# Moving latent rotations, filler units and a key norm in a two-block transformer kernel

## The chip, the core and the metric

The kernel runs on one core of one Trainium2 chip, in one launch. The metric is the device time of a launch in microseconds, median of several runs. Five engines work side by side: TensorE (matmuls, transposes), VectorE, ScalarE, GpSimd and SyncE, which here issues the weight loads. They meet at semaphores only, and each runs its own instructions in order.

## The reference

Two transformer blocks follow each other on 256 tokens of width 2048, all in float32.

- First block: RMS norm, one wide projection, then two attentions side by side. The *compressed/selected/window* attention has 16 query heads in 4 groups of 96 columns, with keys and values shared in a group. The *latent* attention has 16 heads: its queries come from a normed latent of 512 columns through `mla_w_uq`, keys and values from one of 256 columns through `mla_w_uk` and `mla_w_uv`; the last 32 of a head's 96 query columns are rotated by position, and one rotated key part of 32 columns is shared by all heads. Both results are gated and projected; then cross attention to a memory, and a feed-forward part.
- Second block: again a norm and a wide projection; an attention of 8 heads whose queries and keys are normed per head and then rotated, a retention of 8 heads, projections, a gated feed-forward part and a last gated term.

```
q = (rmsnorm(c_q, g_q) @ w_uq).reshape(b, s, MLA_HEADS, MLA_NOPE + MLA_ROPE)
q_rope = apply_rope(q[..., MLA_NOPE:], cos, sin)
k_nope = (ckv @ w_uk).reshape(b, s, MLA_HEADS, MLA_NOPE)
k_r = apply_rope(k_rope, cos, sin)
...
ak = rotate_half_split(heads(rms_norm(ak.reshape(B, T, ATTN_HEADS, HEAD_DIM), k_norm[i])...), pos, inv_freq_attn)
```

## The kernel before

**Matrix products.** Weights arrive in groups of 1 MB (4 row tiles of 128 by 512 columns), 469 in all. For each, ScalarE makes a rounded copy `whi` (`conv`, L1352) and VectorE the rest `wlo` (L1807); two groups fit in `whi` and `wlo`, four in `raw`. TensorE multiplies three times (activation high and low by `whi`, L692 and L693, then high by `wlo`, L697): 24 matmuls of 512 columns per group. Results go to two accumulators `acc`, taken out by ScalarE (`take`, L1385) or VectorE; `acc_free` counts what has been taken. `taken_by(eng, c)` waits until chunk c is out. So each of the three engines has a fixed program in which a group's conversion alternates with other steps; a step is hung in front of a conversion by a hook number.

**Ahead of the first attention.** Three chunks of latent queries `qm` (`C_UQ` to `C_UQ + 2`) are taken by ScalarE, each behind a conversion. Then come two groups of double width, latent keys `kcat` and values `vm`: the first half of each is taken by ScalarE (`two`), the second by VectorE (`second_half`, L1985), which converts a group behind each. `kr_rope` (L1974) rotates the shared key part.

**First attention.** `plan_items` lists 44 items: *prep* (transposes of queries or keys of a group of heads, L923), *attn* (scores of two heads, L941, then exponentials on ScalarE, L1573, transposes of probabilities, L960, value products, L996) and *cmp* (compressed part). Items 3 to 8 are the first group of heads, 9 to 15 the second, 16 to 22 the third, 23 to 29 the fourth (each begins with a prep of the next but one), 30 to 43 the latent heads. TensorE's, ScalarE's and VectorE's programs walk the same list: in step m they do the front of item m, the transposes of item m - 2 and the value products and outputs of item m - 3 (`DEPTH = 3`). A prep or a score product may overwrite its accumulator only once the item two fronts earlier is released; the first two wait for the chunks of `vm` instead.

Between items TensorE gets *filler units*: a projection that has nothing to do with the attention, cut into 32 units of six matmuls of 256 columns (`unit`, L881). `fill_plan` says how many units follow which item. Eight units use up one weight group; when its last unit is done, ScalarE and VectorE convert the group after next in two halves (`conv_half`), in the two items that follow. On VectorE `attend` also runs `mla_operands` (L2002) ahead of three items, 17, 19 and 21:

```
qr = qm[:, :, :].rearrange("p t (h d) -> p t h d", d=DK)
if t < TT:
    for c in (C_UQ + 1, C_UQ + 2):
        taken_by(dve, c)
    c_, s_ = (cs[n][:, t:t + 1, :].to_broadcast([P, HEADS, bh]) for n in ("cosb", "sinb"))
    rope(qr[:, t, :, NOPE:NOPE + bh], qr[:, t, :, NOPE + bh:DK], c_, s_, scratch(rtmp2, HEADS, bh))
    return
linked()
dve.wait_ge(mm_done, 35)
V.tensor_copy(kcat[:, :, :, NOPE:DK], kr.unsqueeze(2).to_broadcast([P, TT, HEADS, ROPE])).then_inc(mla_ready, 1)
```

A rotation (`rope`) is six instructions, L1869 to L1875. The first latent prep is item 23 and waits for `mla_ready`.

**Second block.** The projection's chunks c = 2 to 13 of four groups each carry steps of VectorE, numbered n = 4 c + j: the table `norms` (L2416) hangs `head_product` (squares), `head_sums` (sum, mean, reciprocal) and `norm2` on them. `norm2` has four steps: times the root, times the gain, rotation of tokens 0 to 127, rotation of tokens 128 to 255. Queries are n = 20 to 23, keys 24 to 27. ScalarE takes the root in between (`qk_root`). At n = 28 TensorE transposes the first two heads (`moba_turn`, L1184, L1169), which waits for `qk_ready`, set by the last rotations.

## Time and profile before

| what | value |
|---|---|
| median of 3 runs | 2829.67 us (2828.91 to 2829.94) |
| profiled execution | 2828.72 us, its span 2826.9 us |
| TensorE matmul busy | 2807.8 us, 99% |
| VectorE, ScalarE busy | 1476.9 us (52%), 1223.3 us (43%) |
| mean granted clock of TensorE | 0.995 |
| whole conversion, ScalarE and VectorE | 1.92 us, 2.29 us |
| half conversion, ScalarE and VectorE | 1.07 us, 1.22 us |
| copy of the shared key part (L2013) | 0.69 us |

Three views are used. The list of waits says for which instruction of which engine another one waited. The timeline shows instructions in order of time; in brackets stands how long the engine had been idle and what released it. Windows sum the busy time of each engine between two times and give TensorE's granted clock as a share of 2.4 GHz, so that 0.50 is its lower level of 1.2 GHz. All times count from the span's start.

### The profile page before, as it was taken

The page shows a single profiled execution, that of the slowest core. Times are in us where ns is not written, and L with a number is a line of the kernel's source. Part 1 is how long each engine was busy: PE and PEld are TensorE (multiplying, and loading weights), DVE is VectorE, ACT ScalarE, POOL GpSimd, SP SyncE. Part 2 cuts the span into 40 slices and gives each one's busy share as a digit, 9 for nine tenths or more (in the row PEclk, how much of TensorE's full clock was granted, in tenths as well). Part 3 has the DMA queues.
Part 4 walks back from the last instruction along what each step waited for, and adds up shares of the span by engine and source line. Part 5 has one row for each costly group of instructions (what it writes and reads, how often), then busy time and mean ns, then how long its engine had stood idle before and what let it go on. Part 6 is the DMA issues. An engine that isn't in the chain of part 4 may idle for free.

```text
span 2826.9 us, 32393 instructions
## 1 busy us (share of the span) xinstructions
PE 2807.8 (99%) x13433; PEld 2347.7 (83%) x13433; DVE 1476.9 (52%) x1187; ACT 1223.3 (43%) x1271; POOL 14.7 (1%) x28
## 2 busy tenths in 40 slices
PE   9999999999999999999999999999999999999999
PEld 7888898888888888888888888888888888888887
DVE  4445655445555544454455675665545444445555
ACT  5436454445554334343344544344433333333443
POOL 0000000000000000000000000000000000000000
PEclk9999999999999999999999999999999999999999
DMA  7745015556555565555655654545655555555554
GB/s 253 218 133 179 31 54 185 193 188 215 179 164 181 191 193 182 193 190 190 193 182 186 216 193 148 171 157 179 212 186 187 193 193 193 186 193 188 192 179 149
DMA packets 256429, 508.00 MB, mean 180 GB/s; under 512 B 8163, under 2 KB 18993, under 8 KB 255409
## 3 DMA queue, kind: packets, MB, share of 16 engines
q1 hardware_dynamic: 254112, 495.61, 53.5%
q0 software_dynamic: 2016, 10.36, 1.1%
q8 instruction: 95, 1.56, 0.2%
q10 hardware_dynamic: 176, 0.23, 0.0%
q14 instruction: 30, 0.24, 0.0%
HBM read 504.08 MB, written 2.10 MB: 179 GB/s over the span
## 4 chain that ended last, share of the span: by engine, by line
PE 86%; DVE 1%; ACT 0%; issue 0%; ACTq 0%
PE acc L692 26%; PE acc L693 26%; PE acc L697 26%; PE tb L678 2%; PE tb L996 1%; PE acc L941 1%; PE tb L1179 0%; ACT whi L1352 0%; DVE wlo L1807 0%; PE tb L960 0%; PE acc L894 0%; PE acc L891 0%; PE acc L893 0%; PE tb L1169 0%; PE acc L923 0%
## 5 line engine op out<-in xcount | busy, mean ns | idle before, releaser
L1807 DVE TENSOR_TENSOR wlo<-raw,whi 128x2048 fp32r<-128x2048 f32 (+1 forms) x465 | 1064.8, 2290 | 1228.6 <-ACT whi L1352 1228.4
L1352 ACT ACTIVATE whi<-raw 128x2048 fp32r<-128x2048 f32 (+1 forms) x465 | 890.4, 1915 | 1471.6 <-PE acc L697 1465.9
L692 PE MATMUL acc<-whi,ahi 128*128 128x512 f32 (+1 forms) x1968 | 770.0, 392 | 0.4 <-DVE alo L1899 0.4
L693 PE MATMUL acc<-whi,alo 128*128 128x512 f32 (+1 forms) x1968 | 764.2, 389 | 0.0
L692 PE MATMUL acc<-whi,bhi 128*128 128x512 f32 x1528 | 597.3, 391 | 0.5 <-DVE blo L1837 0.3
L693 PE MATMUL acc<-whi,blo 128*128 128x512 f32 x1528 | 594.7, 389 | 0.0
L697 PE MATMUL acc<-wlo,ahi 128*128 128x512 f32 (+1 forms) x1968 | 484.2, 387 | 0.0
L692 PEld LDWEIGHTS acc<-whi,ahi 128*128 128x128 f32 x1968 | 372.0, 189 | 76.0 <-DVE wlo L1896 0.9
L693 PEld LDWEIGHTS acc<-whi,alo 128*128 128x128 f32 x1968 | 372.0, 189 | 74.4
L697 PEld LDWEIGHTS acc<-wlo,ahi 128*128 128x128 f32 x1968 | 367.1, 188 | 75.5
L697 PE MATMUL acc<-wlo,bhi 128*128 128x512 f32 x1528 | 377.8, 389 | 0.0
L692 PEld LDWEIGHTS acc<-whi,bhi 128*128 128x128 f32 x1528 | 286.9, 188 | 60.7 <-DVE blo L1837 1.2
L697 PEld LDWEIGHTS acc<-wlo,bhi 128*128 128x128 f32 x1528 | 286.8, 188 | 59.6
L693 PEld LDWEIGHTS acc<-whi,blo 128*128 128x128 f32 x1528 | 287.0, 188 | 58.6
L1862 DVE TENSOR_TENSOR h<-acc,h 128x1024 f32<-128x1024 f32 x40 | 48.7, 1218 | 6.4 <-PE acc L697 6.4
L692 PE MATMUL acc<-whi,mhi 128*128 128x512 f32 x128 | 50.2, 392 | 0.0
L693 PE MATMUL acc<-whi,mlo 128*128 128x512 f32 x128 | 49.8, 389 | 0.0
L941 PE MATMUL acc<-kT,qT 96*128 96x128 f32 (+1 forms) x192 | 46.4, 363 | 1.8 <-ACT prob L1573 1.8
L1573 ACT ACTIVATE prob<-acc,negmax 128x128 f32<-128x128 f32 x96 | 39.0, 420 | 8.3 <-DVE negmax L2039 8.3
L2039 DVE TENSOR_REDUCE negmax<-acc 128x2 f32<-128x256 f32 (+1 forms) x48 | 25.2, 554 | 25.9 <-PE acc L944 25.9
L1541 ACT ACTIVATE probT<-tb 128x384 f32<-128x384 f32 x24 | 11.8, 491 | 56.5 <-PE tb L960 56.5
L1406 ACT ACTIVATE junk<-h 128x512 bf16<-128x512 f32 x56 | 35.5, 633 | 1.2
(341 smaller groups left out, 1592.0 us busy)
## 6 DMA issues: line engine op xcount, KB each, us to landing
raw<-in_w_ff SPq DMA_DIRECT2D x128, 1024.0 KB, 5.1
raw<-in_w_in SPq DMA_DIRECT2D x119, 1024.0 KB, 5.1
raw<-in_w_gate SPq DMA_DIRECT2D x44, 1024.0 KB, 5.1
raw<-in_w_up SPq DMA_DIRECT2D x44, 1024.0 KB, 5.1
raw<-in_w_down SPq DMA_DIRECT2D x44, 1024.0 KB, 5.0
raw<-in_w_out SPq DMA_DIRECT2D x16, 1024.0 KB, 5.1
raw<-in_w_o SPq DMA_DIRECT2D x16, 1024.0 KB, 5.0
raw<-in_w_ple_gate SPq DMA_DIRECT2D x16, 1024.0 KB, 5.1
```

The costliest lines, as they stand in the source:

```text
L678: last = nc.tensor.transpose((into or tb[w.n["turn"] % 2])[:, n * P:(n + 1) * P], src, ident)
L692: nc.tensor.matmul(out_(t), hi[:, kt, tt(t)], whi[:, slot, wc(k)], start=first and k == 0, stop=False)
L693: nc.tensor.matmul(out_(t), lo[:, kt, tt(t)], whi[:, slot, wc(k)], start=False, stop=False)
L697: mm = nc.tensor.matmul(out_(t), hi[:, kt, tt(t)], wlo[:, slot, wc(k)], start=False, stop=last and k == len(kts) - 1)
L941: nc.tensor.matmul(o[:, at:end], q[:, t * P:(t + 1) * P], k[:, 0:nk], start=True, stop=False)
L996: last = nc.tensor.matmul(o, probT[:, p % 2, n, b * P:(b + 1) * P], value_of(it, hd, BLOCKS[f][b][1]), start=b == bs[0], stop=b == bs[-1])
L1352: nc.scalar.activation(whi[:, g % SPLIT, 0:n_], raw[:, g % RAW, 0:n_], ACT.Copy).then_inc(w_hi, 1)
L1406: nc.scalar.activation(junk[:, 0:src.shape[-1]], src, ACT.Square, accum_out=ssq[:, r, t, n:n + 1]).then_inc(ssq_done, 1)
L1573: last = nc.scalar.activation(prob[:, p % 2, n, at:end], s[:, n * COLS + c0:n * COLS + c1], ACT.Exp, bias=negmax[:, p % 2, n * TT + t:n * ...
L1807: V.tensor_tensor(wlo[:, g % SPLIT, 0:n_], raw[:, g % RAW, 0:n_], whi[:, g % SPLIT, 0:n_].bitcast(F32), ALU.subtract).then_inc(w_lo, 1)
L1862: V.tensor_tensor(h[:, :, col(n)], v2(s[:, :]), h[:, :, col(n)], ALU.add).then_inc(done, 1)
L2039: last = V.tensor_reduce(negmax[:, p % 2, :].rearrange("p (n t) -> p n t", t=TT)[:, :, t], src, AX.X, ALU.max, negate=True)
```

## The change

Six edits, none of which alters a computed value; the instructions are the same but for their order and waits.

1. `fill_plan`: two units are put behind item 4, those behind items 33 and 37 go. Groups of units thereby end at items 5, 15 and 29 instead of 7, 19 and 33, and half conversions follow them.
2. ScalarE takes the third chunk of `qm` ahead of a conversion instead of behind it (`early`).
3. The latent queries are rotated ahead of the attention: tokens 0 to 127 between the two `second_half` calls, tokens 128 to 255 behind the second.
4. The copy of the shared key part into `kcat` follows its rotation at once.
5. TensorE's first latent prep waits for two counts of `mla_ready`, one from each rotation.
6. `norms`: squares and sums of the keys move from n = 17 and 18 to 16 and 17, query steps from 20 to 23 to 19 to 22, key steps from 24 to 27 to 23 to 26; `qk_root` moves with them.

```diff
--- before.py
+++ after.py
@@ -456,9 +456,9 @@
 
             plan = {m: 1 for m in calls[0] if m < 2 or items[m]["kind"] != "prep"}
             last = calls[0][-1]
-            for m in (last - 15, last - 16, last - 4, last - 2):
+            for m in (last - 15, last - 16, last - 10, last - 6, last - 4, last - 2):
                 del plan[m]
-            plan.update({2: 2, last + 1: 1, last + 2: 1})
+            plan.update({2: 2, 4: 2, last + 1: 1, last + 2: 1})
             assert sum(plan.values()) == FILL_UNITS - 2
             return plan
 
@@ -1014,7 +1014,7 @@
 
                 pe.wait_ge(o_done, items[-1]["u"] + 1)
 
-            attend({("nsa", "q"): (cmp_in, 2), ("mla", "q"): (mla_ready, 1)})
+            attend({("nsa", "q"): (cmp_in, 2), ("mla", "q"): (mla_ready, 2)})
 
 
             def turn_chunk(src, n, c=None, extra=None):
@@ -1484,7 +1484,7 @@
                          3: lambda: (root(R_CQ), root(R_CKV))},
                      ev=lambda: take(lambda t: ga0[:, t, :], ACT.Sigmoid, R_X))
             for n in range(3):
-                block_of(1, ev=lambda: take(lambda t: qm[:, t, col(n)], r=R_CQ))
+                block_of(1, ev=lambda: take(lambda t: qm[:, t, col(n)], r=R_CQ), early=n == 2)
             for t in range(TT):
                 last = nc.scalar.activation(gsig[:, t, :, :].rearrange("p h b -> p (h b)"),
                                             qkv[:, t, O_GN:O_GN + 3 * HEADS], ACT.Sigmoid)
@@ -1738,7 +1738,7 @@
             for c in range(2, 12):
                 hooks = {j: lambda n=4 * c + j: pair_step(n) for j in range(4)}
                 if c == 4:
-                    hooks[3] = qk_root
+                    hooks[2] = qk_root
                 block_of(4, hooks, lambda: take(lambda t: z[:, t, col(c)], r=R_Z))
             for j in range(2):
                 hooks = {i: lambda n=4 * (12 + j) + i: pair_step(n) for i in range(4)}
@@ -1974,6 +1974,9 @@
             def kr_rope():
                 taken_by(dve, 8)
                 rope(kr[:, :, 0:bh], kr[:, :, bh:ROPE], cs["cosb"], cs["sinb"], scratch(rtmp, TT, bh))
+                linked()
+                dve.wait_ge(cmp_h, 2)
+                V.tensor_copy(kcat[:, :, :, NOPE:DK], kr.unsqueeze(2).to_broadcast([P, TT, HEADS, ROPE]))
 
             block_of(2, {1: cmp_out})
             block_of(4, {1: lambda: turn(chi, clo, 0, 4, gT2[:, 0:4]),
@@ -1996,23 +1999,19 @@
                 w.n["used"] += 1
                 w.n["chunk"] += 2
 
+            def query_latent_rope(t):
+
+                qr = qm[:, :, :].rearrange("p t (h d) -> p t h d", d=DK)
+                for c in (C_UQ, C_UQ + 1, C_UQ + 2):
+                    taken_by(dve, c)
+                c_, s_ = (cs[n][:, t:t + 1, :].to_broadcast([P, HEADS, bh]) for n in ("cosb", "sinb"))
+                rope(qr[:, t, :, NOPE:NOPE + bh], qr[:, t, :, NOPE + bh:DK], c_, s_, scratch(rtmp2, HEADS, bh),
+                     by=(mla_ready, t + 1))
+
             second_half(lambda t: kcat[:, t, 8:16, 0:NOPE], R_CKV, lambda s: s.rearrange("p (h d) -> p h d", d=NOPE))
+            query_latent_rope(0)
             second_half(lambda t: vm[:, t, col(1)], R_CKV)
-
-            def mla_operands(t):
-
-                qr = qm[:, :, :].rearrange("p t (h d) -> p t h d", d=DK)
-                if t < TT:
-                    for c in (C_UQ + 1, C_UQ + 2):
-                        taken_by(dve, c)
-                    c_, s_ = (cs[n][:, t:t + 1, :].to_broadcast([P, HEADS, bh]) for n in ("cosb", "sinb"))
-                    rope(qr[:, t, :, NOPE:NOPE + bh], qr[:, t, :, NOPE + bh:DK], c_, s_, scratch(rtmp2, HEADS, bh))
-                    return
-                linked()
-                dve.wait_ge(mm_done, 35)
-                V.tensor_copy(kcat[:, :, :, NOPE:DK], kr.unsqueeze(2).to_broadcast([P, TT, HEADS, ROPE])
-                              ).then_inc(mla_ready, 1)
-
+            query_latent_rope(1)
 
             def o_view(it):
 
@@ -2131,13 +2130,11 @@
                     ins.then_inc(w_lo, 1)
                 w.n["group"] += half
 
-            def attend(between):
+            def attend():
 
                 ms = calls[0]
                 deep = DEPTH
                 for m in range(ms[0], ms[-1] + 1 + deep):
-                    if m in between:
-                        between[m]()
                     if m <= ms[-1]:
                         front_of(m)
                     for step, k in ((end_of, m - deep), (middle_of, m - deep + 1)):
@@ -2150,9 +2147,7 @@
                     if m - 2 in FILL_ENDS:
                         conv_half(1, FILL_ENDS[m - 2])
 
-            at = next(m for m in calls[0] if items[m]["kind"] == "attn" and items[m]["g"] == 2)
-            attend({at + 2 * t: lambda t=t: mla_operands(t) for t in range(TT + 1)})
-
+            attend()
 
             def gates(i, last=False):
                 out_ = lambda: mixed[:, :, col(i) if isinstance(i, int) else ds(i * COLS, COLS)]
@@ -2413,14 +2408,13 @@
                 if n in R_B and R_B[n] < PAIRS:
                     ret_decay(R_B[n])
 
-            norms = {4 * 5 + j: lambda j=j: norm2(0, j) for j in range(4)}
-            norms.update({4 * 6 + j: lambda j=j: norm2(1, j) for j in range(4)})
+            norms = {4 * 4 + 3 + j: lambda j=j: norm2(j // 4, j % 4) for j in range(8)}
             norms.update({
                 4 * 2 + 1: lambda: (dve.wait_ge(con2_in, 16 * 3), taken_by(dve, C_IN2), taken_by(dve, C_IN2 + 1),
                                     head_product(0)),
                 4 * 2 + 2: lambda: head_sums(qss[:, 0, :]),
-                4 * 4 + 1: lambda: (taken_by(dve, C_IN2 + 2), taken_by(dve, C_IN2 + 3), head_product(1)),
-                4 * 4 + 2: lambda: head_sums(qss[:, 1, :], qk_var),
+                4 * 4: lambda: (taken_by(dve, C_IN2 + 2), taken_by(dve, C_IN2 + 3), head_product(1)),
+                4 * 4 + 1: lambda: head_sums(qss[:, 1, :], qk_var),
                 4 * 9 + 2: lambda: (taken_by(dve, C_IN2 + 6), taken_by(dve, C_IN2 + 7), rope2(3, "r", 3, 0)),
                 4 * 9 + 3: lambda: rope2(3, "r", 3, 1),
                 4 * 10 + 1: lambda: (taken_by(dve, C_IN2 + 8), taken_by(dve, C_IN2 + 9), rope2(4, "r", 4, 0)),
```

VectorE, ahead of the first attention (`kcat` latent keys, `vm` latent values, `qm` latent queries, `rtmp` scratch). Before:

```order
L1807 TENSOR_TENSOR wlo<-raw,whi 128x2048 x4
L1993 TENSOR_SCALAR kcat<-acc,rstd 128x8x64 x2
L1807 TENSOR_TENSOR wlo<-raw,whi 128x2048
L1993 TENSOR_SCALAR vm<-acc,rstd 128x512 x2
L1807 TENSOR_TENSOR wlo<-raw,whi 128x2048
L2039 TENSOR_REDUCE negmax<-acc 128x2
```

and after the change:

```order
L1979 COPY kcat<-qkv 128x32x32
L1807 TENSOR_TENSOR wlo<-raw,whi 128x2048 x4
L1996 TENSOR_SCALAR kcat<-acc,rstd 128x8x64 x2
L1807 TENSOR_TENSOR wlo<-raw,whi 128x2048
L1869 TENSOR_TENSOR rtmp_130<-qm,con 128x256
L1870 TENSOR_TENSOR rtmp_130<-qm,con 128x256
L1871 TENSOR_TENSOR rtmp_130<-qm,con 128x256
L1872 TENSOR_TENSOR rtmp_130<-qm,con 128x256
L1874 TENSOR_TENSOR qm<-rtmp_130 128x16x16
L1875 TENSOR_TENSOR qm<-rtmp_130 128x16x16
L1996 TENSOR_SCALAR vm<-acc,rstd 128x512 x2
L1807 TENSOR_TENSOR wlo<-raw,whi 128x2048
```

Six instructions of a rotation stand ahead of the values' copy, and the key copy ahead of the four conversions.

VectorE, opening of the second block's attention (`z` the projection, `negmax` the first maximum of scores). Before:

```order
L1874 TENSOR_TENSOR z<-tmp_98 128x8x64
L1875 TENSOR_TENSOR z<-tmp_98 128x8x64
L1807 TENSOR_TENSOR wlo<-raw,whi 128x2048
L2349 TENSOR_REDUCE negmax<-tb 128x2 x2
L1807 TENSOR_TENSOR wlo<-raw,whi 128x2048 x2
L2356 COPY pT_103<-tb 128x384
L2349 TENSOR_REDUCE negmax<-tb 128x2 x2
L1807 TENSOR_TENSOR wlo<-raw,whi 128x2048
```

and after the change:

```order
L1874 TENSOR_TENSOR z<-tmp_98 128x8x64
L1875 TENSOR_TENSOR z<-tmp_98 128x8x64
L1807 TENSOR_TENSOR wlo<-raw,whi 128x2048 x2
L2344 TENSOR_REDUCE negmax<-tb 128x2 x2
L1807 TENSOR_TENSOR wlo<-raw,whi 128x2048 x2
L2351 COPY pT_103<-tb 128x384
L2344 TENSOR_REDUCE negmax<-tb 128x2 x2
L1807 TENSOR_TENSOR wlo<-raw,whi 128x2048
```

Behind the last rotation there are now two conversions ahead of the first maximum instead of one: the rotation has moved up by a group.

## Rows read from the trace of the kernel before

**Rows 1.** Page, busy totals; TensorE's waits: us in total, times, longest

```profile
PE 2807.8 (99%) x13433; PEld 2347.7 (83%) x13433; DVE 1476.9 (52%) x1187; ACT 1223.3 (43%) x1271; POOL 14.7 (1%) x28
...
PE tb L1169 <- DVE z L1875: 3.3, 1, 3.3
...
PE tb L996 <- DVE probT L2064: 2.9, 4, 1.9
...
PE tb L996 <- DVE qkv L2117: 1.8, 2, 1.3
...
PE acc L941 <- ACT prob L1573: 1.8, 1, 1.8
```

**Rows 2.** First attention, windows: busy us (x instructions) by engine, granted clock, DMA

```profile
281.60:288.52 6.92, 6.92 (x43) 6.53 (x44) 2.68 (x9) 2.81 (x12) 0.00 (x0) 0.75 0.01 2
295.59:305.33 9.74, 9.06 (x73) 8.10 (x71) 7.90 (x19) 5.70 (x18) 0.00 (x0) 1.00 0.32 98
305.33:311.22 5.89, 5.51 (x45) 4.95 (x44) 3.77 (x13) 2.40 (x10) 0.00 (x0) 1.00 0.06 19
346.30:355.37 9.07, 9.07 (x76) 8.53 (x75) 5.83 (x17) 4.77 (x16) 0.00 (x0) 1.00 0.19 75
295.59:318.29 22.70, 21.64 (x171) 19.50 (x170) 15.31 (x41) 11.24 (x42) 0.00 (x0) 1.00 0.15 47
318.29:346.30 28.01, 24.83 (x170) 22.15 (x169) 20.23 (x54) 13.02 (x45) 0.00 (x0) 0.88 0.05 15
375.88:379.90 4.02, 4.02 (x34) 3.71 (x34) 2.68 (x7) 1.71 (x7) 0.00 (x0) 1.00 0.00 0
391.78:395.33 3.55, 3.46 (x29) 2.93 (x28) 2.09 (x5) 1.27 (x5) 0.00 (x0) 1.00 0.00 0
```

**Rows 3.** The same view at the opening of the second block's attention

```profile
1709.36:1717.32 7.96, 7.96 (x32) 6.58 (x33) 2.18 (x1) 1.08 (x2) 0.00 (x0) 0.79 0.51 169
1724.55:1731.56 7.01, 7.01 (x39) 6.03 (x38) 2.76 (x2) 3.26 (x4) 0.00 (x0) 1.00 0.50 168
1725.42:1725.99 0.57, 0.57 (x8) 0.57 (x7) 0.00 (x0) 0.57 (x1) 0.00 (x0) 1.00 1.04 406
```

**Rows 4.** Timelines there: start, us, instruction, [idle before it <- releaser]

```profile
1709.36 1.14 PE L1169 MATMUL tb<-con,z 128*128 128x128 f32 x8 [3.28 <-DVE z L1875]
...
1642.85 2.29 DVE L1807 TENSOR_TENSOR wlo<-raw,whi 128x2048 fp32r<-128x2048 f32 x1 [3.15 <-ACT whi L1352]
...
1648.29 2.29 DVE L1807 TENSOR_TENSOR wlo<-raw,whi 128x2048 fp32r<-128x2048 f32 x1 [3.15 <-ACT whi L1352]
...
1708.53 0.68 DVE L1875 TENSOR_TENSOR z<-tmp 128x512 f32<-128x512 f32 x1
...
1642.72 1.24 ACT L1385 ACTIVATE z<-acc,rstd 128x512 f32<-128x512 f32 x2
```

**Rows 5.** Timelines, opening of the first attention: TensorE, then VectorE

```profile
262.85 0.50 PE L692 MATMUL acc<-whi,chi 128*128 128x512 f32 x1 [0.50 <-ACT qm L1385]
...
272.83 0.64 PE L923 MATMUL acc<-con,qkv 128*96 128x128 f32 x4
...
274.30 1.08 PE L923 MATMUL acc<-con,qkv 128*96 128x128 f32 x8
...
278.41 0.36 PE L891 MATMUL tb<-whi,ahi 128*128 128x256 f32 x1
...
279.21 0.60 PE L923 MATMUL acc<-con,qkv 128*96 128x128 f32 x4
...
267.93 2.29 DVE L1807 TENSOR_TENSOR wlo<-raw,whi 128x2048 fp32r<-128x2048 f32 x1 [0.60 <-ACT whi L1352]
...
271.37 1.41 DVE L1993 TENSOR_SCALAR vm<-acc,rstd 128x512 f32<-128x512 f32 x2 [1.14 <-PE acc L697]
...
322.03 0.41 DVE L1869 TENSOR_TENSOR rtmp<-qm,con 128x256 f32<-128x256 f32 x1
...
324.17 0.42 DVE L2039 TENSOR_REDUCE negmax<-acc 128x2 f32<-128x256 f32 x1
```

## The prediction

> **What bounds the kernel now.** I read the totals first: TensorE carries matmuls in 99% of the span [rows 1]. What a re-ordering can win is the time in which TensorE stands still, and what each such pause does to its clock afterwards. So the second view is the list of TensorE's waits [rows 1]: four entries hold 9.8 us, and each lies where the change works. 3.3 us: the first transposes of the second block's attention (L1169) wait for the last rotation of its keys on VectorE (L1875). 2.9 and 1.8 us: value products of the first attention (L996) wait for VectorE. 1.8 us: a score product (L941) waits for ScalarE's exponentials. There is more than the waits: TensorE's granted clock is 1.00 in most stretches, but 0.75 in the one that begins behind the 1.8 us pause, at 281.60 [rows 1, 2], 0.88 in the third group of heads [rows 2] and 0.79 behind the 3.28 us pause at 1709.36 [rows 3, 4]. These are mixtures of its two levels, 2.4 and 1.2 GHz: TensorE stood, and its clock then fell for some us. A stall is therefore priced as a difference between two stretches with the same instructions, one with and one without it. Ends of windows are starts of TensorE instructions.
>
> **Second block, key norm a group earlier.** A group of weights (24 matmuls of 512 columns) takes 5.44 us, the distance of two conversions on VectorE [rows 4], which converts one per group and does its steps in between. The last key rotation starts its last instruction at 1708.53 and TensorE starts at 1709.36 [rows 4]. All steps from the squares of the keys on move up by one group, so this end moves from 1709.2 to about 1703.8, ahead of 1706.1, where TensorE stood ready (1709.36 less 3.28). What could stop it is the input: the step now at hook 16 needs the second key columns out of the accumulator. ScalarE starts that copy at 1642.72 and is done by 1644.0; VectorE comes to the hook at 1642.85 + 2.29 = 1645.1 [rows 4]. It is there with 1.1 us to spare. Gain: the pause, 3.28, and the clock. From the transposes to the next score product it is 7.96 us at clock 0.79; the same for the next pair is 7.01 at 1.00, in which six more transposes take 0.57 [rows 3]: 7.96 - (7.01 - 0.57) = 1.52. Together **4.8 us**. Nothing new is late: the weight conversion behind the rotation starts at 1703.8 and its product comes two thirds through a group that now begins at 1706.9.
>
> **First attention, latent query copy ahead of a conversion.** ScalarE's third copy goes ahead of a 1.9 us conversion, and the 0.50 us pause at 262.85 [rows 5] ends. The conversion is 1.2 us later, for a group that TensorE wants only at 265.2, after about 262.7. Gain 0.5, carried into the next term.
>
> **First attention, opening.** VectorE now rotates half of the latent queries between conversion and value copy. The conversion starts at 267.93, by the term before at about 267.4, ends 2.29 later at 269.7; the rotation takes 324.17 - 322.03 = 2.14 and a wait for its own write of 0.1, so the value copy that started at 271.37 starts at 271.9 [rows 5]. TensorE's second preparation (keys, 272.83) follows the copy by 1.46: 273.4, a **new wait** of about 1.1 us. The third one stood before for ScalarE and absorbs a part: 274.30 becomes 274.5 [rows 5]. From there on all is 0.2 late, the score product at 281.60 too, with two more filler units in front of it that eat most of its pause (a unit is six matmuls, 279.21 - 278.41 = 0.80 with the switch [rows 5]). From it to the next score product it was 6.92 at clock 0.75; the twin in the second group of heads needs 5.89 at 1.00, with a wait of its own [rows 2]. 5.89 is what I take: 281.8 + 5.89 = 287.7 against 288.52, gain **0.8**, though two units more are done. The second rotation and the key copy (0.69, formerly in the attention) lie in VectorE's idle time and cost nothing. If the copy waited a full rotation, and nothing absorbed it, it would cost 1.6 more; if the third preparation absorbed all, 0.2 less.
>
> A rule weighed against this row: successive rotation instructions start 0.34 apart though each is shown with 0.42, six in 2.14 us [rows 5]. The Trainium skill, VectorE: DVE Perf Modes, section The DRAIN you can't avoid, says that the next operation does not start until the pipe has emptied; by full durations the six would take 2.5 and the opening be 0.4 later, the sum 0.4 smaller. The trace disagrees, and I keep 2.14.
>
> **Second to fourth group of heads.** The units at the opening fill weight groups earlier, so the two half conversions (1.1 to 1.2 us each on ScalarE and VectorE) move: from items 8, 9 to 6, 7; from 20, 21 to 16, 17; from 34, 35 to 30, 31. In items 6 and 7 both engines have idle time, and I take no cost (at worst the 0.67 below). The second group loses its halves: its first part takes 9.74 with them, the same part of the fourth group without them 9.07 [rows 2], gain **0.67**. The third group takes 28.01 against 22.70 for the same work in the second [rows 2]: two rotations of 2.14 and the key copy sat on VectorE there. They are gone, and its half conversions come in at an earlier place. Free of all it would take 22.70 - 0.67 = 22.03; with the halves at worst 22.70. I take the middle, 22.37: one of the two falls into the wait for the value product. Gain **5.64** (5.3 to 6.0). The fourth group itself is unchanged, and behind it, at items 30 and 31, come halves that were not there: cost 0 to 0.67, taken as **-0.3**.
>
> **Units taken away.** Items 33 and 37 lose a unit. The stretch with a unit is 4.02, without it 3.55 [rows 2]: VectorE's copy of the probabilities is ready soon after. 2 x 0.47 = **0.94** (0 to 1.6). The sum of units is unchanged, and their cost at the opening is already in.
>
> **The sum.** 0.83 + 0.67 + 5.64 - 0.3 + 0.94 = 7.8 for the first attention, 4.8 for the second block: 12.6 us. The profiled execution, 2828.72 (span 2826.9), would be 2816.1; the median is 0.95 above it: 2829.67 - 12.6 = **2817.1**, ratio 0.9955.
>
> The clock makes nearly half of this: 1.5 in the second block, some 3 in the third group (a mean of 0.88 means 6.7 of 28 us at the lower level, at 0.46 each as under (d)), about 1 in the opening.
>
> **Rivals.** (a) *The clock falls again at the opening.* The new wait of 1.1, then 0.5 and 0.4 lie within 13 us. For: a pause of 1.8 was followed by a fall, and so was that of the third group. Against: each new one is shorter. Price 1.5 in the opening, to 3.4 where it lasts as in the third group: 2818.6 to 2820.5. (b) *The attention stays bound by VectorE's chain*, and the gain of the third group is given back wait by wait; only the second block and 0.5 to 1 us remain: 2829.7 - 5.5 = 2824.2. Against: the second group does the same work in 22.70. (c) *The key norm doesn't come up*, since its input is late, with the rest as forecast: 2829.7 - 7.8 = 2821.9. Against: 1.1 us of slack. (d) *Slower: the clock falls at the new wait of 1.1 us and stays down.* From 273 on short waits follow each other every few us; if each keeps the clock at its lower level until the next, TensorE runs slowly from 273 to the end of the second group near 318, 45 us. Behind 1709.36 a mean of 0.79 in 7.96 us means 3.3 us at the lower level, which cost 1.52: 0.46 us for each us there [rows 3]. 45 x 0.46 = 20.7: 2837.8. It decides from 12.6 / 0.46 = 27 us at the lower level. Against: waits like those in the second group, which together take about a microsecond there, leave it at clock 1.00 [rows 2]. (e) *The waits go, the clock's losses stay*: it falls as often, in other places. Then the sum is 12.6 - 5.6 = 7.0 and the time 2822.7. Against: windows with equal instructions and waits below half a microsecond show 1.00 [rows 2]. The Trainium skill, TensorE: Matmul & The Clock Gate, section The HAM clock gate, advises to leave such ramps out of a model, being under 1% of a span, which gives the same 2822.7; but here the whole change is worth 0.4%, and the rows show the ramps' price.
>
> **How the numbers follow.** Forecast with its terms' bounds, 2814.5 to 2818.6: 0.60. (a) 0.17, (b) 0.09, (c) 0.05, (d) 0.05, (e) 0.04. The range for eight in ten takes the forecast, (a) and (c), and below it the upper bounds of the third group and the units with half a microsecond between runs: 2813.5 to 2822.5. A measurement of this kernel tells about 0.2%, 5.7 us, from no change: faster means under 2824.0. The forecast, (a), (c) and (e) are faster, 0.86, and (b) in a fifth of its cases: 0.88. Same 0.07, slower 0.05.
>
> **What would show it.** After: no wait of L1169 for L1875, and clock 1.00 behind it; the pause at 262.85 gone; a wait of about 1.1 us of TensorE for the value copy near 273; the pause of the second score product down from 1.8 to about 0.5, and clock 1.00 there; the third group near 22.4 us at clock 1.00; a few waits of 0.2 to 0.5 at L996 left. A clock below 1.00 anywhere between 271 and 340 says (a); L996's waits for VectorE still at 4 us or more in sum say (b); a mean clock under 0.8 over tens of us says (d). I would be wrong above all if short pauses that follow close on each other pull the clock down as one long one does.

## The result, and the profile of the changed kernel

| | before | changed kernel |
|---|---|---|
| median of 5 runs | 2828.91 us (2828.00 to 2829.94) | 2814.62 us (2812.82 to 2814.87) |
| profiled execution | 2828.72 us, span 2826.9 | 2812.82 us, span 2811.0 |
| mean granted clock of the span | 0.995 | 0.999 |

The ratio is 0.9946, 95% interval 0.9935 to 0.9958. The forecast was 2817.1 us in a range of 2813.5 to 2822.5, faster with 0.88: the sign and the range held, and the median is 2.5 us below the forecast.

The totals and TensorE's waits of the changed kernel, against [rows 1] (columns of the waits: us in total, times, longest):

```profile
PE 2798.9 (100%) x13433; PEld 2341.2 (83%) x13433; DVE 1477.0 (53%) x1187; ACT 1223.8 (44%) x1271; POOL 14.7 (1%) x28
...
PE tb L996 <- DVE probT L2063: 1.7, 5, 0.4
...
PE acc L923 <- DVE vm L1996: 0.9, 1, 0.9
...
PE acc L941 <- ACT prob L1573: 0.4, 1, 0.4
```

The wait of L1169 (3.3 us) is gone, L941's is 0.4 instead of 1.8, and of the 4.7 us that L996 waited for VectorE 1.7 are left, none longer than 0.4. One wait is new: 0.9 us for the value copy, where about 1.1 was foreseen. All other engines do the same work as before. TensorE's busy time fell as well, by 8.9 us with the same 13433 matmuls: that is nearly all the clock (busy time in the third group alone 24.83 to 21.48, in the opening 6.92 to 5.61, behind the second block's transposes 7.96 to 6.33, in the compression the 2.46 below).

The windows that answer to [rows 2] and [rows 3] (columns: length, TensorE busy with its instructions, granted clock, DMA share, GB/s):

```profile
279.14:285.07 5.93, 5.61 (x43) 1.00 0.01 3
292.14:314.06 21.92, 21.46 (x171) 1.00 0.09 36
314.06:336.18 22.12, 21.48 (x170) 1.00 0.14 49
365.81:369.36 3.55, 3.46 (x29) 1.00 0.71 213
1695.07:1701.40 6.33, 6.33 (x33) 1.00 0.57 174
```

In this order they stood at 6.92, 22.70, 28.01, 4.02 and 7.96 us, three of them at a clock of 0.75, 0.88 and 0.79. Now every one is at 1.00.

The timeline of the opening, against [rows 5] (start, us, instruction, idle before it and what ended it):

```profile
267.91 1.03 PE L923 MATMUL acc<-con,qkv 128*96 128x128 f32 x8
...
270.60 0.64 PE L923 MATMUL acc<-con,qkv 128*96 128x128 f32 x4 [0.95 <-DVE vm L1996]
271.80 1.03 PE L923 MATMUL acc<-con,qkv 128*96 128x128 f32 x8
...
279.14 0.51 PE L941 MATMUL acc<-kT,qT 96*128 96x143 f32 x2 [0.43 <-ACT prob L1573]
...
266.88 0.42 DVE L1869 TENSOR_TENSOR rtmp<-qm,con 128x256 f32<-128x256 f32 x1
...
269.13 1.41 DVE L1996 TENSOR_SCALAR vm<-acc,rstd 128x512 f32<-128x512 f32 x2
```

And the second block, TensorE and VectorE, against [rows 4]:

```profile
1695.07 1.03 PE L1169 MATMUL tb<-con,z 128*128 128x128 f32 x8
...
1692.24 0.69 DVE L1875 TENSOR_TENSOR z<-tmp 128x512 f32<-128x512 f32 x1
```

The last key rotation starts its last instruction 2.8 us ahead of the transposes that need it; before it was 0.8, with TensorE waiting.

**Where the time went.** The start of the same TensorE instruction in both traces, subtracted, gives the gain up to that place. It is 2.46 us already at the first group that multiplies the normalised latents (243.16 before, 240.70 after), and the change touches nothing ahead of that. Before, then in the changed kernel:

```profile
243.16 0.39 PE L692 MATMUL acc<-whi,chi 128*128 128x512 f32 x1
...
240.70 0.39 PE L692 MATMUL acc<-whi,chi 128*128 128x512 f32 x1
```

Then it is 3.26 at the first preparation (271.17, 267.91), 3.45 at 288.52 (285.07), 4.23 at 318.29, 10.12 at 346.30, 10.85 at 406.41 (395.56), 11.01 just ahead of the second block's transposes without their pause, 15.92 at the score product behind them (1717.32, 1701.40), and 15.9 at the end. So the change itself is worth 15.92 - 2.46 = 13.5 us in this pair of traces; the forecast was 12.6. The other 2.46 us lie in a stretch that no prediction spoke of, the compression. Before, the two stretches behind its small matmuls:

```profile
185.93:194.11 8.18, 8.18 (x27) 0.67 0.23 89
200.96:208.37 7.41, 7.41 (x26) 0.73 0.17 66
```

and in the changed kernel, the same instructions:

```profile
185.56:192.35 6.79, 6.79 (x26) 0.82 0.29 113
199.15:205.91 6.76, 6.76 (x25) 0.81 0.20 79
```

TensorE is fully busy in both, and yet the clock falls, for longer in the one trace than in the other. It falls already within the rows of small matmuls, as their own windows show, the keys' and the values', before and then in the changed kernel:

```profile
178.80:185.93 7.13, 7.13 (x66) 0.90 0.66 192
194.11:200.96 6.85, 6.85 (x66) 0.79 0.30 85
...
178.62:185.56 6.94, 6.94 (x65) 0.93 0.64 191
192.35:199.15 6.80, 6.80 (x66) 0.94 0.27 78
```

How long it stays down isn't the change's doing: the kernel of the experiment e8, whose code up to there is the same as the changed kernel's, shows 0.67 and 0.73 behind the rows too, and the changed kernel's own second trace (after_again) 0.78 and 0.80. The five runs of the changed kernel fall in two clusters: 2812.82, 2812.85 with a mean clock of 0.999, and 2814.62, 2814.65, 2814.87 with 0.997. Only one of the five has a trace, so that these stretches part the clusters is inferred. e8 speaks for it: its trace has both falls long, one part of the change is undone that is worth 0.81 us, and 2815.99 - 0.81 = 2815.2. The kernel before spreads wider, from 2823.4 to 2831.0 us in the 62 fast runs that were taken beside the experiments, at mean clocks of 0.997 to 0.994; the compression explains 2.5 us of that, and no trace shows the rest.

### The profile page after: what moved, and what is told of

Same layout as the page of the kernel before. It is cut to its first block, busy times and chain, and to the rows that moved or that the text cites. A ratio compares the mean times of both kernels' runs of the same rounds, so it can differ in the third digit from the quotient of the medians.

```text
span 2811.0 us, 32396 instructions
## 1 busy us (share of the span) xinstructions
PE 2798.9 (100%) x13433; PEld 2341.2 (83%) x13433; DVE 1477.0 (53%) x1187; ACT 1223.8 (44%) x1271; POOL 14.7 (1%) x28
## 4 chain that ended last, share of the span: by engine, by line
PE 98%; DVE 1%; ACT 1%; issue 0%; ACTq 0%; DVEq 0%
PE acc L692 29%; PE acc L693 29%; PE acc L697 29%; PE tb L678 2%; PE acc L941 1%; PE tb L996 1%; PE tb L816 0%; PE tb L960 0%; ACT whi L1352 0%; PE acc L923 0%; PE tb L1179 0%; PE acc L894 0%; PE acc L891 0%; PE acc L893 0%; PE tb L1169 0%
## 5 line engine op out<-in xcount | busy, mean ns | idle before, releaser
L941 PE MATMUL acc<-kT,qT 96*128 96x128 f32 (+1 forms) x192 | 44.8, 354 | 0.4 <-ACT prob L1573 0.4
```

The source lines that it names most:

```text
L941: nc.tensor.matmul(o[:, at:end], q[:, t * P:(t + 1) * P], k[:, 0:nk], start=True, stop=False)
```

## The experiments

Ten kernels ran, and the changed kernel a second time. The diffs are against the kernel before for e1 to e4, against the changed kernel for the rest. Each was timed against the kernel before on the same chip (median there 2828.84, 2828.99 and 2829.41 us in the three sets).

### One part at a time

**e1_norm_only**: the second block's part alone.

```
-                    hooks[3] = qk_root
+                    hooks[2] = qk_root
...
-            norms = {4 * 5 + j: lambda j=j: norm2(0, j) for j in range(4)}
-            norms.update({4 * 6 + j: lambda j=j: norm2(1, j) for j in range(4)})
+            norms = {4 * 4 + 3 + j: lambda j=j: norm2(j // 4, j % 4) for j in range(8)}
...
-                4 * 4 + 1: lambda: (taken_by(dve, C_IN2 + 2), taken_by(dve, C_IN2 + 3), head_product(1)),
-                4 * 4 + 2: lambda: head_sums(qss[:, 1, :], qk_var),
+                4 * 4: lambda: (taken_by(dve, C_IN2 + 2), taken_by(dve, C_IN2 + 3), head_product(1)),
+                4 * 4 + 1: lambda: head_sums(qss[:, 1, :], qk_var),
```

> The kernel before with one part of the change alone: the norm of the second block's keys, its sums and its roots a group of weights earlier. The first attention stays as it was. Theory: the second block's part is independent of the rest, so TensorE's wait of L1169 for L1875 (3.28 us) goes and the granted clock behind it is 1.00 instead of 0.79; in the pair of before and after this stretch gave 5.07 us, so 4.8 to 5.1 us less than before, about 2824. Rival (the clock falls there without the pause, as it did in the compression): the wait goes but the clock stays low behind the transposes, 3.3 us less, about 2825.5. Rival (the norm comes no earlier, or another wait ends there): under 1 us less. The first attention should show its waits of before (2.9 us of L996 for L2063, 1.8 us of L941).

Measured: 2823.28 us median, ratio 0.9982 (0.9973 to 0.9991); profiled 2823.46, which is 5.3 less than the trace of before. The wait is gone and the clock behind is 1.00, and the same 6.33 us as in the changed kernel stand between the transposes and the score product:

```profile
1705.76:1712.09 6.33, 6.33 (x34) 1.00 0.59 176
```

The waits of the first attention stayed at 2.9 and 1.8 us. The part is independent, and the rival with a low clock without a pause is out.

**e2_rotations_only**: the rotations and the key copy ahead of the attention; no filler moved, ScalarE's third copy not early.

```
+            query_latent_rope(0)
             second_half(lambda t: vm[:, t, col(1)], R_CKV)
-
-            def mla_operands(t):
...
+            query_latent_rope(1)
...
-            at = next(m for m in calls[0] if items[m]["kind"] == "attn" and items[m]["g"] == 2)
-            attend({at + 2 * t: lambda t=t: mla_operands(t) for t in range(TT + 1)})
-
+            attend()
```

> The kernel before with the rotations of the latent queries and the key copy ahead of the first attention, and nothing else: the filler units stay in their old places, the third latent query copy of ScalarE stays behind its conversion, and the norm of the second block stays where it was. Theory: the third group of heads loses its two rotations, its key copy and its loss of clock, while its half conversions stay: from 28.0 us to about 22.7, 5.3 less. Against it at the opening: a rotation of 2.1 us on VectorE ahead of the value copy, so a wait of TensorE near its second preparation of 1.0 to 1.5 us, with no more filler to cover the pause behind; the pause of the score product (1.8 us) and the low clock behind it stay. Together 4 to 5.5 us less than before, about 2824.5. Rival (the pause of 1.8 grows by the shift or the clock falls earlier): the opening loses 1 to 1.5 us more, 3 to 4 us less in all. Rival (VectorE's chain is late in the third group anyway): under 2 us less.

Measured: 2824.04 us median, ratio 0.9986 (0.9977 to 0.9995); profiled 2823.29. Of these 5.4 us, 2.4 are the compression's luck (its clock behaved as in the changed kernel's trace); from there to the second block's transposes (1704.16 against 1709.36) the gain is only 2.8. The opening, the stretch to the third group, and the third group:

```profile
279.99:288.58 8.59, 8.59 (x42) 0.60 0.01 2
...
318.56:341.14 22.58, 21.67 (x170) 1.00 0.07 11
```

The third group gives 28.01 - 22.58 = 5.4, as expected. But the opening loses 2.5 us from the first preparation to 288.58. 0.8 of it is the new wait. The rest is the clock: the pause ahead of the score product is still there, at 279.99, and the stretch behind it, 6.92 us at 0.75 before, is 8.59 at 0.60. The rival that had the opening lose more (3 to 4 us in all) came nearer than my 4 to 5.5.

```profile
271.46 0.64 PE L923 MATMUL acc<-con,qkv 128*96 128x128 f32 x4 [0.94 <-DVE vm L1996]
...
279.99 0.70 PE L941 MATMUL acc<-kT,qT 96*128 96x143 f32 x2 [1.86 <-ACT prob L1573]
```

The second pause is 1.86 against 1.79. Two pauses within 9 us and a longer time at the lower level is what rival (a) described; with one trace of each I can't say whether the first pause or the moment of the second made it longer.

**e3_filler_only**: the plan of the filler units alone.

```
-            for m in (last - 15, last - 16, last - 4, last - 2):
+            for m in (last - 15, last - 16, last - 10, last - 6, last - 4, last - 2):
...
-            plan.update({2: 2, last + 1: 1, last + 2: 1})
+            plan.update({2: 2, 4: 2, last + 1: 1, last + 2: 1})
```

> The kernel before with the filler plan of the change alone: two filler units taken from items 33 and 37 and put at the opening, half conversions six or two items earlier as a result. The rotations and the key copy stay in the third group of heads. Theory (terms add up): opening 0.8 to 1.5 us less, because 1.6 us of matmuls fill most of the 1.8 us pause and the clock holds; second group 0.7 less; third group 0 to 0.7 more, since its half conversions now meet the rotations; the two units at the end 0.7 to 0.9 less. Together 1.5 to 2.5 us less than before. Rival (the units only pay together with the rotations, since the halves land on the rotations in the third group and the clock falls there for longer): third group 2 us longer, no difference in all or up to 1 us more.

Measured: 2824.16 us median, ratio 0.9987 (0.9978 to 0.9996); profiled 2824.14. 4.6 us less than the trace of before, 0.9 of them in the compression, so 3.6 for the plan, more than the 1.5 to 2.5 expected. By parts:

```profile
280.69:286.62 5.93, 5.60 (x42) 1.00 0.01 3
...
315.62:342.52 26.90, 24.49 (x170) 0.87 0.12 41
```

Opening 1.0 (the pause is 0.36 and the clock holds), second group 0.8, third group 1.1, behind it 0.7. The third group is what I had wrong: I expected the half conversions in their earlier place to collide with the rotations there, and TensorE's idle time in it went down from 3.2 us [rows 2] to 2.4. Its clock still falls, behind one wait of 2.4 us:

```profile
PE tb L996 <- DVE qkv L2117: 2.4, 1, 2.4
```

**e8_late_copy**: the changed kernel without the early copy of ScalarE.

```
-                block_of(1, ev=lambda: take(lambda t: qm[:, t, col(n)], r=R_CQ), early=n == 2)
+                block_of(1, ev=lambda: take(lambda t: qm[:, t, col(n)], r=R_CQ))
```

> The changed kernel with one part undone: ScalarE's copy of the third latent query chunk stands behind its conversion again. Theory: the pause of 0.50 us of TensorE at the first value product of weights comes back and everything behind is 0.5 us late; VectorE's first rotation still finds its input. 0.5 us more than the changed kernel, about 2815.1. Rival (the pause behind it absorbs it, because the value copy and not TensorE sets the second preparation): the pause comes back but the wait for the value copy shrinks from 0.95 to about 0.45: no difference. Rival: the conversion is then earlier and something gains: up to 0.3 us less.

Measured: 2815.93 us median (2815.39 to 2816.02), ratio 0.9959 (0.9945 to 0.9972). Its trace has the two long falls in the compression, and all five runs have the clock 0.997, so they are to be compared with the changed kernel's runs at that clock, 2814.6 to 2814.9: about 1 us more. The trace says how much: it is 2.38 us behind the changed kernel's at the first group of the latents (243.08 against 240.70), and 3.19 at the first preparation (271.10 against 267.91). The copy is worth 0.81 us, although the pause is shown with 0.50:

```profile
262.78 0.50 PE L692 MATMUL acc<-whi,chi 128*128 128x512 f32 x1 [0.50 <-ACT qm L1385]
```

The wait for the value copy stayed at 0.9, so nothing absorbed it; both rivals are out.

### The clock behind a pause

**e4_cover_the_pause**: the kernel before, with 24 matmuls whose result nothing uses, where TensorE stood for 3.28 us.

```
+                    for _ in range(24):
+                        nc.tensor.matmul(tb[1][:, 0:SEQ], ahi[:, 0, 0:P], ahi[:, 1, :], start=True, stop=True)
```

> The kernel before with 24 more matmuls of 256 columns on TensorE right ahead of the second block's first transposes, where it stood for 3.28 us; their result is used by nothing, so they are work added. VectorE's order is the one of before: the key rotation still ends at about the same time. 24 matmuls of 256 columns are about 2.7 us at full clock. Theory (the 1.5 us behind that pause are the clock's, which falls because TensorE stood): the pause shrinks to about 0.6 us, the transposes start at the same time as before, the granted clock in the stretch behind them is 1.00 instead of 0.79, and that stretch takes 6.4 us instead of 8.0: 1.5 us less than before, although work was added. Rival (what follows is slow for another reason, such as waits or the transposes themselves): no gain, the stretch stays at 8.0 us. Rival (the added matmuls themselves run into a fall of the clock and overrun the pause): 0 to 2 us more.

Measured: 2827.09 us median against 2828.84, 1.75 less with work added; the ratio's interval (0.9988 to 1.0006) doesn't exclude no change, but the two traces show the place. The added matmuls, the transposes, and the stretch to the score product:

```profile
1705.83 3.03 PE L1189 MATMUL tb<-ahi 128*128 128x256 f32 x24
1709.18 1.09 PE L1169 MATMUL tb<-con,z 128*128 128x128 f32 x8 [0.32 <-DVE z L1877]
```

```profile
1709.18:1715.59 6.41, 6.41 (x32) 1.00 0.56 189
```

The transposes start 0.18 earlier than in [rows 4], and what follows takes 6.41 instead of 7.96 at clock 1.00 instead of 0.79. VectorE was as late as before. So the 1.5 us that I had put down to the clock are the clock's (7.96 - 6.41 = 1.55), and here it falls because TensorE stood.

### Beyond the change: the new wait and the compression

**e5_rotation_earlier**: the first rotation ahead of the third conversion.

```
-            for _ in range(3):
+            for _ in range(2):
                 block_of(1)
+            query_latent_rope(0)
+            block_of(1)
...
-            query_latent_rope(0)
             second_half(lambda t: vm[:, t, col(1)], R_CKV)
```

> The changed kernel with one step moved: the rotation of the first half of the latent queries stands on VectorE ahead of the last of the three conversions of the query chunks (where VectorE stood still for 4.2 us), no longer between the conversion and the value copy. Theory: the new wait of 0.95 us of TensorE for the value copy is the rotation's doing and goes; nothing else takes its place, since the step ends (about 260.7) just as ScalarE's conversion comes (260.3). 0.7 to 0.95 us less than the changed kernel's 2814.6, about 2813.8, and in the trace a distance of 1.7 instead of 2.7 us between the first and the second preparation. Rival: the gain is absorbed by the next wait, the score product's for ScalarE's exponentials, which grows from 0.43 to about 1.2 us: under 0.3 us less. Rival: the conversion behind the rotation comes 0.4 us late and TensorE waits for it: 0.4 us more.

Measured: 2813.98 us median (2812.53 to 2814.50), ratio 0.9952 (0.9938 to 0.9965). The medians say little: the five runs fall in the two clusters again, 2812.53 and 2812.66, then 2813.98 to 2814.50, against 2812.82 and 2812.85, then 2814.62 to 2814.87 of the changed kernel, and its second timing, on the chip of this run, has its median at 2813.05. The trace shows the place:

```profile
268.44 1.03 PE L923 MATMUL acc<-con,qkv 128*96 128x128 f32 x8
270.10 0.64 PE L923 MATMUL acc<-con,qkv 128*96 128x128 f32 x4
271.58 1.08 PE L923 MATMUL acc<-con,qkv 128*96 128x128 f32 x8
```

The wait is gone, 1.03 us are won at the second preparation and 0.28 given back at the third: 0.75, at the score product still 0.72. The rotation was the cause of the wait. It came later than I had expected, and the conversion behind it started at 261.49 instead of 260.32, but TensorE did not wait for it.

**e6_compression_mixed**: the compression's products among the matmuls of 512 columns, two behind each of 16.

```
                 for k, kt, t in tiles:
                     nc.tensor.matmul(out_(t), hi[:, kt, tt(t)], whi[:, slot, wc(k)], start=first and k == 0, stop=False)
+                    few()
                     nc.tensor.matmul(out_(t), lo[:, kt, tt(t)], whi[:, slot, wc(k)], start=False, stop=False)
+                    few()
...
-            chunk(ahi, alo, hook={2: lambda: cmp_first(0), 3: lambda: cmp_first(1)})
+            chunk(ahi, alo, mix={2: lambda: cmp_first(0), 3: lambda: cmp_first(1)})
```

> The changed kernel with the two times 32 products of the compression (60 columns each, two instructions apiece, 14 us in two dense rows) spread, two behind each of the first 16 matmuls of 512 columns of the same two groups of weights; the sums are the same. Theory (the granted clock falls behind these dense rows of small matmuls although TensorE never stands, once behind each row, and how long it stays down differs from run to run): mixed with large ones the clock stays at 1.00 from 178 to 206 us, 3.1 us less for the two falls in the trace of the changed kernel, up to 6 where both are long; about 2811, runs of one kernel closer together. On top comes between 0 and 6 us less if a small product costs its columns alone beside a large one, instead of 0.11 us an instruction. Rival: the fall has nothing to do with the row of small matmuls: the two low stretches stay at the same place, within 1 us of the changed kernel. Rival: every change between small and large costs something that the dense rows saved, some 0.06 us times 64: 2 to 4 us more, which eats the clock's gain.

Measured: 2820.72 us median, ratio 0.9977 (0.9968 to 0.9986): 6.1 us more than the changed kernel, worse than the worst rival. The keys' part, the start of the values' part (four pairs of one large matmul and four small instructions, and one large matmul more), the rest of it up to the last eight large matmuls, and those with what follows:

```profile
178.72:191.10 12.38, 12.38 (x90) 1.00 0.53 169
191.10:195.28 4.18, 4.18 (x22) 1.00 0.01 4
195.28:210.56 15.28, 15.28 (x61) 0.50 0.21 69
210.56:219.10 8.54, 8.54 (x36) 0.50 0.02 1
```

The keys' part is as hoped: no fall, and 12.38 us, the sum of a group (5.44) and the dense row (178.62 to 185.56 in the changed kernel, 6.94). That row holds the start of a fall, though; in after_again, where it fell later (clock 0.98 in the row), it took 6.74, so spreading the keys' products cost 0.2 us, and nothing is won by a small product running beside a large one. The values' part is another matter. From one large matmul to the next, with four small instructions between them, it takes 0.96 us at clock 1.00, where with the keys' it is 0.66:

```profile
185.54 0.58 PE L824 MATMUL tb<-k2T,w1k 96*96 96x60 f32 x4
185.89 0.47 PE L696 MATMUL acc<-whi,alo 128*128 128x512 f32 x1
...
186.55 0.47 PE L694 MATMUL acc<-whi,ahi 128*128 128x512 f32 x1
...
191.41 0.61 PE L824 MATMUL tb<-v1T,w1v 64*64 64x60 f32 x4
191.95 0.49 PE L696 MATMUL acc<-whi,alo 128*128 128x512 f32 x1
...
192.91 0.51 PE L694 MATMUL acc<-whi,ahi 128*128 128x512 f32 x1
```

What differs is the tile: 96 by 96 for the keys, 64 by 64 for the values, between large ones of 128 by 128. Each pair of steps to and from a 64 by 64 tile costs 0.3 us; whether its rows or its columns count, no run separates. (The 0.4 in the expectations of e9 and e10 divides the 4.18 us by four, though the window holds a fifth large matmul.) Then the clock falls, and it stays down behind the spread part as well, through large matmuls and narrower ones. This trace is of a run of 2823.4 us, from the slower of two clusters (2820.3 to 2821.8 and 2823.4 to 2823.5). In the trace of e7 (2819.77 us) the clock is at 0.50 from 196.0 to 213.0 and at 1.00 from there.

**e7_both**: e5 and e6 together.

```
+            query_latent_rope(0)
+            block_of(1)
...
+            chunk(ahi, alo, mix={2: lambda: cmp_first(0), 3: lambda: cmp_first(1)})
```

> The changed kernel with both edits: the first rotation ahead of the last query conversion and the compression's products spread among the large ones. They lie 60 us apart on TensorE and touch different waits, so the theory has their gains add up: 0.7 to 0.95 and 3.1 or more, about 2810. Rival: no gain over the better one of the two.

Measured: 2820.01 us median, ratio 0.9975 (0.9966 to 0.9984): 0.71 under e6, the 0.72 that the trace of e5 shows. The gains add; the total missed with e6.

**e9_keys_mixed**: e5, with only the keys' products mixed.

```
+            chunk(ahi, alo, hook={3: lambda: [f() for f in cmp_first(1)]}, mix={2: lambda: cmp_first(0)})
```

> The changed kernel with the first rotation ahead of the last query conversion, and of the compression's products only those of the keys spread among the large ones; those of the values stay one dense row. In the run with both spread, the keys' part took 12.38 us at clock 1.00, just the sum of a group (5.44) and the dense row (6.94), while in the values' part each pair of changes cost about 0.4 us and the clock fell for long. Theory (only the 64-row products pay for being mixed; a dense row of 96-row ones costs the clock alone): the fall behind the keys' row goes, that behind the values' row stays: 1.0 to 1.6 us less than the kernel with the rotation alone, about 2812.7, and the clock 1.00 from 178 to 198. Rival: the fall only moves behind the values' row and lasts longer there: within 0.3 us of the kernel with the rotation alone.

Measured: 2811.24 us median (2810.70 to 2812.31), ratio 0.9939 (0.9925 to 0.9952). That is 2.7 under e5's median, more than expected, but e5's median stands in its upper cluster; the two profiled runs differ by 1.45 (2811.21, 2812.66), as expected.

```profile
178.70:191.17 12.47, 12.47 (x90) 1.00 0.53 168
191.17:198.04 6.87, 6.87 (x65) 0.71 0.28 81
198.04:204.97 6.93, 6.93 (x26) 0.79 0.19 73
```

One fall is gone, the one of the values' row stays. As in the other traces it begins inside the row, here earlier (clock 0.71 in the row), with TensorE busy all the way; the row takes 6.87 us, where it took 6.80 at clock 0.94 in the changed kernel. So in these 64 by 64 products the lower clock cost next to nothing, and the price of a fall depends on what it meets.

**e10_values_in_four_rows**: e9, and the values' products in four rows of eight.

```
+                def few():
+                    passed[0] += 1
+                    if mixed_in and passed[0] % every == 0:
+                        for _ in range(2 * every):
...
+                             mix=mix[j] if j in mix else None, every=4 if j == 3 else 1).then_inc(mm_done, 1)
```

> As the run before, and the values' products in four rows of eight behind every fourth large matmul, instead of one row of 32. From the run with both spread, a pair of changes between these products and large ones costs about 0.2 to 0.4 us; three more of them are 0.6 to 1.2 us. Theory (the clock falls behind a long row): no fall any more, 1.6 to 3.1 us back, so 0.5 to 2 us less than with the keys alone spread, about 2811.5. Rival (every step between the two shapes is itself what pulls the clock down, whatever the rows' length): it falls again and longer, as with both spread: 2 to 5 us more.

Measured: 2810.73 us median, ratio 0.9936 (0.9922 to 0.9949), and the five runs lie between 2810.53 and 2810.88.

```profile
178.80:191.20 12.40, 12.40 (x90) 1.00 0.52 169
...
191.20:204.64 13.44, 13.44 (x89) 1.00 0.25 79
```

No fall is left in the trace. The values' part is 13.44 us against some 12.2 for a row of 6.8 and a group of 5.44: 1.2 more, of which three more pairs of steps at e6's 0.3 are 0.9. Against e9's 6.87 + 6.93 = 13.80 it wins 0.36, and 0.51 by the medians: at the lower end of what was expected, since that fall had cost less than the theory had it. The kernel has the lowest median of those here, though the runs of e9 overlap with it, and its runs agree within 0.35 us where those of the changed kernel differ by 2.

**after_again**: the changed kernel on the chip of e9 and e10.

> The changed kernel itself, as the measure for the two others on the same chip: 2812.8 to 2814.9, in two clusters.

Measured: 2813.05 us median (2812.92, 2813.05, 2813.05, 2814.96, 2815.20), ratio 0.9948 (0.9934 to 0.9961). e10 is 2.3 us below it. The two clusters are there again, with the median now in the lower one.

## Why the prediction was right, point by point

Measured gains are differences of starts between the two traces, as above.

| term | forecast | measured |
|---|---|---|
| latent query copy ahead of a conversion | 0.5 | 0.80 |
| opening, to the score product at 288.52 | 0.33 more (0.83 with the copy) | 0.19 |
| second group of heads | 0.67 | 0.78 |
| third group | 5.64 | 5.89 |
| halves behind the fourth group, units away | 0.64 | 0.73 |
| second block | 4.8 | 4.91 |
| not placed (between 406 and 1695) | 0 | 0.16 |
| sum | 12.6 | 13.5 |
| compression, untouched | 0 | 2.46 |

- **Second block.** Right in mechanism and size, and shown by e1 (the part alone) and e4 (the clock alone). The pause gave 3.28, the clock 7.96 - 6.33 = 1.63 where I took 1.52.
- **Latent query copy.** The mechanism was right, the term was too small: I took the idle time shown, 0.50, and e8 against the changed kernel gives 0.81. Behind the group's last matmul the next starts 1.57 us after the start of its last row of four in e8, 0.91 in the changed kernel; that is 0.66, and the first group behind the pause takes 0.15 longer to come back to its pace.
- **Opening.** The new wait of 0.95 (forecast 1.1), the third preparation absorbing 0.27 of it, the pause of 0.43 (forecast 0.5) and the 5.93 us at clock 1.00 (forecast 5.89) are all there. What I could not see from the sum is that the filler was the condition: e2 loses 2.5 us here without it. The parts don't add. Opening: -2.5 (rotations alone), +1.0 (filler alone), +0.8 (copy), and +1.0 together. Third group: +5.4 and +1.1 alone, 5.9 together.
- **Third group.** 22.12 us between the bounds of 22.03 and 22.70. With the half conversions left in their old place (e2) it is 22.58, so their earlier place is worth 0.46, where the middle value had taken 0.33.
- **Units.** 4.02 became 3.55 us, exactly the row of a stretch without a unit [rows 2]; with the halves' cost the term is within 0.1.
- **The rotations' pitch.** In the changed kernel the six rotation instructions and what follows them start as in [rows 5]: from 266.88 to the value copy at 269.13 it is 2.25, the 2.14 and the wait of 0.1 of the forecast. The Trainium skill, VectorE: DVE Perf Modes, section The DRAIN you can't avoid, as the prediction read it, would have had the copy 0.4 later, and the trace disagrees here too. But the same paragraph of the page says that a next operation that is not held starts earlier, so the page as a whole is not contradicted; the prediction had left that sentence out.
- **Rivals.** (a) no clock below 1.00 between 262 and 357. (b), (c) and (d) left no sign. (e) is refuted by the windows of the changed kernel, all at 1.00, and the price of a fall by e4, about 1.5 us for one. The Trainium skill, TensorE: Matmul & The Clock Gate, section The HAM clock gate, puts the ramp penalty at under 1% of a typical span; the falls that went were some 6 us of 2827 here, which agrees, and yet they are over a third of the change.
- **What failed.** The step "half a microsecond between runs". It took the runs shown of before as the spread, and priced the clock only where TensorE had stood. The trace of before held two more stretches with a low clock, 0.67 and 0.73, behind the compression, and I did not look there, as the change didn't touch it. With both long, as in the trace of before, the changed kernel is 2828.72 - 13.5 = 2815.2, and its slower cluster is there (2814.6 to 2815.2). The forecast's miss of 2.5 us has three parts: 0.9 in the terms, most of it the copy and the third group; 0.95 in the start, since I took the median of three runs of before, 2829.67, to lie that much above its trace, and five runs had 2828.91; 0.6 between 2815.2 and the measured median.
- **What was luck.** The low end of the range, 2813.5, was too high. Two of the five runs lie under it (2812.82, 2812.85), and so does the median of the second timing, 2813.05. That the first median stands inside comes of three runs of five falling in the upper cluster.

## What to carry to other kernels

Price a pause of TensorE by two stretches with the same instructions, one behind the pause and one without it: in this kernel the clock added 1.63 us to a pause of 3.28, about 1.0 to one of 1.79 (6.92 against 5.93) and 2.66 to one of 1.86 (e2, 8.59 against 5.93), so it can cost more than the pause itself. Covering the pause of 3.28 with matmuls whose result nothing used gave the clock's part back. Before moving work ahead of a stage, look for a longer pause further down that the move doesn't cure, because the parts of such a change don't add: the rotations gave 5.4 us in their old place and lost 2.5 in the new one until filler covered it. And read the granted clock of the whole span, also where the change does nothing, since that is where the runs of one kernel part.

## What the runs showed of the hardware that was not expected

- The granted clock fell in dense rows of small matmuls although TensorE never stood: 64 instructions of 60 columns at 0.11 us each, 0.71 to 0.98 in the row itself, then 0.67 to 0.82 in the group behind. How long it stayed down differed between traces of one kernel; the traces of before and of the changed kernel differ by 2.46 us through it. With the rows broken up among large matmuls (e10) the traced run shows 1.00 throughout.
- A step between a 128 by 128 and a 64 by 64 tile and back cost 0.3 us at full clock, one between 128 and 96 next to nothing (16 of them 0.2 us). Sixteen such pairs to 64 by 64 close together (e6, e7) held the clock at 0.50 for 17 us and more with TensorE shown as fully busy. Whether it is the steps' hidden idle time that the clock answers to was not tried.
- Single pauses of 1.79 (before, opening), 1.86 (before, third group; e2, opening), 2.41 (e3) and 3.28 us were each followed by a fall; one of 1.27 in the third group of before (clock 1.00 up to 333.70) and one of 0.95 in the changed kernel were not. No run tries the lengths between.
- A pause shown with 0.50 us cost 0.81.
